# Products that nobody reads between the output projection and the experts of a hybrid encoder layer

## What is computed

```
z = rms_norm(x) @ w_in                              # 1024 -> 1536
y_pool = pooling mixer(z[:, :512])                  # windows 2, 4, 8, 16
y_conv = swish(layer_norm(causal_conv31(value * sigmoid(gate))))
x = x + concat(y_pool, y_conv) @ w_out + b_out      # output projection
h = rms_norm(x)
g_sel = top 1 of 4 groups (h @ w_rg + b_rg); eid = top 2 of 8 experts in that group (h @ w_re + b_re)
x = x + sum over the two experts e of gate_e * (silu(h @ w_eg[e]) * (h @ w_eu[e])) @ w_ed[e]
y = rms_norm(x)
```

## Time and profile before

| | |
|---|---|
| median of three runs | 1084.33 us |
| profiled execution, its own time | 1084.51 us |
| its span, first to last instruction | 1082.8 us |
| TensorE busy | 933.9 us, 86% of the span |
| VectorE busy | 877.2 us, 81% |
| ScalarE busy | 622.4 us, 57% |
| mean granted TensorE clock | 0.927 of full speed |

### The profile page before, as it was taken

How to read it: one execution, slowest core, us unless ns; L and a number is a source line. 1 busy time by engine, 2 the same in 40 slices (tenths; PEclk the granted TensorE clock), 3 DMA queues, 4 the chain that set the end, 5 groups by cost and what they waited for, 6 DMA issues and landing times.

```text
span 1082.8 us, 13490 instructions
## 1 busy us (share of the span) xinstructions
PE 933.9 (86%) x4446; PEld 766.9 (71%) x4446; DVE 877.2 (81%) x974; ACT 622.4 (57%) x592; POOL 262.3 (24%) x284
## 2 busy tenths in 40 slices
PE   4999999791699983979999999999999999999710
PEld 3788888570468872768888888888888888888500
DVE  6279998979647875989898989898988989898248
ACT  7245353530232222747878787878787878887223
POOL 2158688350001101032212121212121111111000
PEclk8999999996889985889999999999999999999865
DMA  8211111131116242789999999999999999999466
GB/s 262 84 53 35 37 35 59 26 112 39 74 43 233 107 175 85 239 295 391 375 390 375 395 382 398 389 386 387 382 384 373 386 380 385 375 385 349 158 271 232
DMA packets 66299, 268.63 MB, mean 248 GB/s; under 512 B 15215, under 2 KB 28015, under 8 KB 40601
## 3 DMA queue, kind: packets, MB, share of 16 engines
q1 hardware_dynamic: 56761, 250.36, 61.9%
q0 software_dynamic: 9504, 17.85, 4.3%
HBM read 254.09 MB, written 30.86 MB: 263 GB/s over the span
## 4 chain that ended last, share of the span: by engine, by line
PE 81%; DVE 8%; issue 4%; ACT 3%; DMA 2%; SPq 0%; DVEq 0%; POOLq 0%; POOL 0%; ACTq 0%
PE ps L1021 11%; PE ps L1023 11%; PE ps L1022 11%; PE ps L899 8%; PE ps L1035 6%; PE ps L1036 6%; PE ps L1037 6%; PE ps L779 5%; PE ps L780 5%; PE ps L781 5%; PE ps L1010 3%; DVE arena L1496 2%; DVE ps L1155 2%; PE ps L1042 1%; PE ps L954 1%
## 5 line engine op out<-in xcount | busy, mean ns | idle before, releaser
L704 ACT ACTIVATE big<-arena 128x2048 fp32r<-128x2048 f32 x192 | 363.1, 1914 | 70.6 <-PE ps L1037 36.9
L1431 DVE TENSOR_TENSOR low<-arena,big 128x2048 fp32r<-128x2048 f32 x126 | 285.2, 2286 | 39.9 <-ACT big L704 37.2
L1021 PE MATMUL ps<-big,ring 128*128 128x512 f32 x512 | 205.5, 401 | 2.4 <-DVE ring L1436 2.4
L1023 PE MATMUL ps<-big,ring 128*128 128x512 f32 x512 | 201.2, 393 | 0.0
L1431 DVE TENSOR_TENSOR big<-arena,big 128x2048 fp32r<-128x2048 f32 x66 | 151.0, 2289 | 18.1 <-ACT big L704 14.7
L1155 DVE SCALAR_TENSOR_TENSOR ps<-arena,cols,ps 128x512 f32<-128x512 f32 (+1 forms) x174 | 137.2, 788 | 6.0
L1021 PEld LDWEIGHTS ps<-big,ring 128*128 128x128 f32 x512 | 97.0, 189 | 22.6 <-DVE ring L1436 2.8
L1023 PEld LDWEIGHTS ps<-big,ring 128*128 128x128 f32 x512 | 96.8, 189 | 22.5
L899 PE MATMUL ps<-big,ring 128*128 128x512 f32 (+1 forms) x432 | 104.7, 402 | 8.4 <-ACT arena L591 3.9
L1035 PE MATMUL ps<-big,hT 128*128 128x512 f32 x256 | 103.0, 402 | 8.9 <-DVE hT L1446 8.9
L779 PE MATMUL ps<-big,ring 128*128 128x512 f32 (+1 forms) x288 | 104.0, 361 | 0.4 <-DVE big L1119 0.4
(11 more groups left out here) (228 smaller groups left out, 1409.2 us busy)
## 6 DMA issues: line engine op xcount, KB each, us to landing
arena<-in_w_eg SPq DMA_DIRECT2D x64, 1024.0 KB, 7.6
arena<-in_w_eu SPq DMA_DIRECT2D x64, 1024.0 KB, 7.0
arena<-in_w_ed SPq DMA_DIRECT2D x64, 1024.0 KB, 7.2
arena<-in_x_prompt SPq DMA_DIRECT2D x16, 512.0 KB, 5.4
y_in<-y_scratch SPq DMA_DIRECT2D x8, 1024.0 KB, 12.7
arena<-in_w_in SPq DMA_DIRECT2D x12, 512.0 KB, 3.6
arena<-in_w_out SPq DMA_DIRECT2D x8, 512.0 KB, 4.0
x_scratch<-arena SPq DMA_DIRECT2D x8, 512.0 KB, 2.6
```

What stands on the lines that cost most here:

```text
L704: act.activation(we_h[n % RING], raw[n % RING], ACT.Copy).then_inc(high_done, 1)
L1021: pe.matmul(out, part_h[b][:, k, :], wh[:, q, :], start=(k == 0), stop=False)
L1023: ins = pe.matmul(out, part_l[b][:, k, :], wh[:, q, :], start=False, stop=(k == KD - 1))
L1431: dve.tensor_tensor(we_l[n % RING], raw[n % RING], we_h[n % RING].bitcast(F32), ALU.subtract).then_inc(low_done, 1)
```

## The change

A helper `spin(n)` issues n float32r products of 128 x 128 by 128 x 512, each with start and stop, into bank 4. Nobody reads the results, no semaphore is waited for and none is raised. It is called in TensorE's stream at five places: behind `ranks(6)` (6 products), behind `ranks(7)` (10), behind `ranks(8)` (4), behind the last products of the slot table (36), and between `turn_rows(0)` and the wait for the split rows (8). That makes 64 products. The other engines' streams are as they were.

```diff
+            def spin(n):
+                for _ in range(n):
+                    pe.matmul(banks(4, 1), part_l[1][:, 0, :], part_l[1][:, 0:4, :], start=True, stop=True)
...
                     slot_table("own", 0, 2 * NT - 6)
                 if t >= 3:
                     ranks(t - 3)
+                if t >= NT:
+                    spin((6, 10, 4)[t - NT])
             slot_table("own", 2 * NT - 6, 2 * NT)
+            spin(36)
...
             turn_rows(0)
+            spin(8)
             pe.wait_ge(xe_low, 1)
             expert_in(-1, 0, gate_ps)
```

## The result

The changed kernel took 1078.82 us (median of 6, 1077.35 to 1080.15) against 1084.2 us before (median of 6 in the same comparison). The ratio is 0.9949, 95% interval 0.9936 to 0.9962: 5.4 us faster. Forecast were 1082.4 us and a range from 1080.7 to 1084.6. The direction came out, and so did the clock's rise at the turn and the first expert; 5.4 us is far more than the 3.84 us that the prediction had as its gross gain.

The account below looks back on a forecast made before the run. TensorE was taken as the bound, 81% of the span, with low-clock slices round 400 to 480 us reachable. From 1084.51 us, - 3.84 + 1.5 + 0.3 = - 2.0, less 0.1 left out, gave 1082.4 us; range 1080.7 to 1084.6.

Parts of the forecast that it names:

- gross gain: At the first turn and first expert, full clock from the start was to save 2.90 plus 0.94, 3.84 us.
- the expert's term: The first expert's 24 products were to take 5.58 us at the upper clock instead of 8.48: 2.90 us gained.
- the turn's 0.94: The turn of eight on TensorE was to take 1.03 us at the upper clock instead of 1.97.
- rival E: A typical execution loses less at the first expert: term 1.7 us, not 2.9; time 1083.6 us, chance 0.16.
- D = 1.5 us: Ten products behind `ranks(7)` were to delay `ranks(8)`, making `place(8)` and the gather late by 1.5 us, bounds 0 and 1.8.
- Rival A: Nothing is late: the clock rises in the first two fillers, the ten take 2.3 us; 1080.9 us, chance 0.18.
- The 36 behind the slot table: They were to fill TensorE's 11.02 us wait for the gather in 9.9 to 11.1 us, costing 0, at most 0.3.
- The eight: Products behind the turn, 1.83 us at the upper clock in a 2.34 us wait: no cost.
- The overflow table: At `slot_table("over")` TensorE was still to come last, after VectorE, with 0.6 us of cover, so the gain stays.
- The second gather: Started by the end of the first turn; TensorE was not to wait for it, at worst 1.6 us.
- The second low stretch: At 470.7 to 474.4 us, without filler, the low clock was to cost 0.3 us more, bounds 0 and 1.2.
- Rivals B, C and D: B: VectorE or second gather late, 1083.7, 0.12; C: clock down at turn, 1086.0, 0.08; D: clock never lifted, 1091.7, 0.02.

Follow-up runs that it names:

- e1_layout_only: The changed kernel with all 64 added products 32 columns wide instead of 512, same instruction count: 1081.3 us, ratio 0.9965 to the kernel before.
- e4_first_three: The changed kernel with its last two groups (36 and 8) 32 columns wide, first three kept at 512: 1081.83 us, ratio 0.9971 to the kernel before.
- e3_last_two: The changed kernel with its first three groups (6, 10, 4) 32 columns wide, last two kept at 512: 1078.87 us, ratio 0.9949 to the kernel before.

## Why the prediction was wrong
**The step that failed** is the sentence that from 490 us on the change "touches nothing there, it can only shift this stretch as a whole". It costed the 128 added instructions by their time where they run, and not by where they put the code behind them. TensorE's stream leaves the loop over pairs through a second loop of 8 turns, each of which branches over a body of 358 instructions that it skips. The idle time there depends on where 16384-byte fetches fall: 6.2 to 7.5 us with two fetches, 3.2 to 3.3 with one. That was 3.0 of the 5.4 us by the exits, and 3.8 by the ratio of the kernel with 100 increments, whose interval is 1.4 us to either side. It is shown with no added product at all (100 increments: 0.9965; 64: 1.0001). The Trainium skill (Runtime: NRT & Kernel Launch, Instruction fetch mechanics) says that each engine's instructions come in blocks of 16 KiB, that the fetching is sequential, and that a taken branch to a block that isn't there waits for its fetch. The traces agree: in all thirteen profiles queue 8 has one packet of 16384 bytes at the exit where it is short, and two where it is long, the second 3.1 to 3.7 us behind the first. Why a long exit is 6.2 us in one profile and 7.5 in another stays open. That two fetches stand one after the other because start and end of the skipped body, 360 instructions apart, then lie two blocks apart is inferred from my count; the runs show the dependence, not the blocks.

The profile before had it in view: a row of 6.22 us "issue" in the chain, which I had seen and taken for a constant. With its 3.0 us the sum of 1082.4 would have been 1079.4, 0.6 us from the measured time, but by luck: three other terms were off and made up for each other, as follows.

**The clock's gross gain, 3.84 us.** From the first turn to the second the pair of profiles shows 3.79, so the working was right for this pair. But the profiled execution before was an unlucky one there, in two ways. Its first expert took 8.48 us to the second turn, where four profiles without the higher clock there have 7.1 to 7.7 (7.28 with 64 increments), a fifth (128 increments) 8.2, and the filled ones 5.6. And its gather took 9.26 us, the longest of thirteen (the others 7.6 to 9.2), which the prediction read as the room for the 36. Together, from `s_idx` to the second turn, the same four have 21.0 us (64 increments, 419.91 to 440.91), 21.3 (100 increments), 21.5 (e1_layout_only) and 21.4 (e4_first_three), against 23.35 (442.49 less 419.14). The filled ones took 18.2 to 19.5. The two ends with 64 increments, VectorE's cast and TensorE's second turn:

```profile
419.91 0.18 DVE L1378 CAST s_idx<-idx_f 128x32 uint32<-128x32 f32 x1
```

```profile
440.91 1.03 PE L1013 MATMUL ps<-ident,arena 128*128 128x128 f32 x8
```

So the expert's term was 1.5 to 2.1 us in four profiles and 2.6 in the fifth, where the prediction had 2.9, and with the turn's 0.94 the gross gain was typically 2.4 to 3.0: rival E was right on this term (it had 1.7). Its argument against, that the execution lay only 0.18 over the median, was false comfort: this execution had gained about 1.5 us in the stages ahead (419.14 us at `s_idx`, where the other twelve profiles have a median of 420.7), which hid it. The warning of the Trainium skill (TensorE: Matmul & The Clock Gate, Part 1) that the prediction cites, not to fit to one count of slow products, would have been the better guide.

**D = 1.5 us, the late `ranks(8)`.** It was 0, in all four profiles that have the ten products. Rival A was right on this term: the clock came up just behind the first six (408.6 us; 408.3, 407.2 and 406.7 in the others), so the logits and the table ran faster, and the ten took 2.6 to 4.1 us; `ranks(8)` then waited for `count(8)` (1.65 us idle) or came in time. My argument against A, that only small products stand between, overlooked that it could rise on the six.

**The 36 behind the slot table.** The prediction put their cost at 0, with 0.3 as the bound. Their own length came out as worked out (10.96 us for at most 11.1), but the room did not: the gather landed earlier than in the profile before, and they cost 1.3 us in the changed kernel's profile and 0 to 1.1 in the five others with 36.

The errors, 1.5 us too much cost for `ranks(8)`, some 1 too much gain at the expert and up to 1.3 too little cost for the 36, all but cancelled: the clock's net, forecast 1.9 to 2.0, came out as 1.5 to 2.4. That is luck.

**The eight** fit (0.55 us to spare behind them). **The overflow table** stayed TensorE's: VectorE waited 0.83 us for it, forecast 0.6 (for D = 1.8). **The second gather** was not waited for. **The second low stretch** cost 0.65 us more in this profile (12 products at 0.43 us for 9), forecast 0.3. In the profiles that leave it unfilled, with the change or without, the count is 9 to 14 (13 and 14 in the two with increments ahead of the loop over the blocks), so nothing here puts the 12 down to the change. Filling it took 2.4 us off, as the prediction's arithmetic would have said had it asked for that.

Rivals B, C and D did not happen. The time of an expert in the loop was 17.89 us in the changed kernel's profile and 17.91 before (0.57 us in all). I had put that to the position; it isn't, since e3_last_two and e4_first_three have the changed kernel's position and 17.91. What sets it stays open.

## What to carry to other kernels
Adding or removing instructions moves all code behind them. Where an engine's stream has loops or skipped branches, look for "issue" time in the chain at their ends and for the instruction queue's packets, and before a gain is put down to the work that was added, run it with the same number of instructions and no work. Filling TensorE's waits pays only where TensorE is the next in the chain, and only as far as the filler ends before what is waited for: the room must be read from several executions, since this gather took 7.6 to 9.3 us. And here 44 products at two waits did as much as 64 at five. Price the term from several executions where the clock is in it: one profile can be 2 us off for a stretch while the total looks typical.

## What the runs showed that I had not expected
- An increment of a semaphore in TensorE's stream costs 0.14 to 0.15 us (17.8 and 19.14 us for 128).
- A float32r product of 32 columns takes 0.21 us at the lower clock (7.84 us for 36), half of one with 512 columns (0.43 us): narrow products are no cheap filler.
- Leaving a loop into one that is skipped 8 times costs TensorE 3.2 us at best and up to 7.5 us.
